# Two weight splits, one wide matmul: the FFNs of a four-block float32 stack with both operand parts in one 512-column matmul

## The chip, the core and the metric

The kernel runs on one core of a Trainium2 chip. The metric is the device time of one execution in microseconds. All work is in float32 accuracy, made out of matmuls on a reduced-precision operand type (float32r).

## The reference

Two blocks of two layers each, on 256 tokens of width 1024. Every layer is a mixer (retention with pooling, conformer convolution, short convolution, windowed attention) and then a SwiGLU FFN of inner width 2816:

```python
def swiglu(h, w_gate, w_up, w_down):
    return (jax.nn.silu(h @ w_gate) * (h @ w_up)) @ w_down

for layer in range(DEPTH):
    hn = rms_norm(h, mixer_norm_g[layer])
    h = h + mixer(hn, ...)
    h = h + swiglu(rms_norm(h, ffn_norm_g[layer]), ffn_w_gate[layer], ffn_w_up[layer], ffn_w_down[layer])
```

There are four FFNs in all; the change concerns them.

## The kernel before

**Layout.** Activations stand transposed: 128 features on the partitions, 256 tokens on the free axis; `h` has 8 such pieces, the FFN's inner activations 22. Weights come in tiles of 128x128, and all weights of the program lie in one array in the order in which they are used, 2944 tiles; 528 of them belong to each FFN: 352 for gate and up, 176 for down.

**Three products per tile.** A float32 product is made of three float32r ones. A weight piece (8 tiles, 1024 columns) arrives by DMA, ScalarE rounds it to `hi_t` (`split_hi`, L278), VectorE writes the rest, raw minus hi, to `lo_t` (`split_lo`, L284). An activation is split likewise, into `xh` (ScalarE, L305) and `xl` (VectorE, L309), inside an FFN into `fh` (L508) and `fl` (L469). `tile` issues three 256-column matmuls into one half of a PSUM bank: hi weight by high activation (L353), hi weight by low activation (L356), lo weight by high activation (L359). The lo by low product is left out.

**An FFN.** Up: group u (of 22) is 16 tiles, gate part in the first half of a bank and up part in the second, banks 0, 1, 6, 2 in turn (`UP_BANKS`). The first two groups are worked through together, by k. VectorE evicts a group with one 128x512 multiply by the broadcast of the RMS norm (L480), which frees the bank (semaphore `s_up`); ScalarE takes silu of the gate half (L516); VectorE multiplies by the up half (L465, called `gate`); ScalarE rounds to `fh` (L508, `high`); VectorE makes `fl` (L469, `low`), one group later. Down: block n (of 8) is 22 tiles, one for each inner piece, banks 3, 4, 5 in turn; VectorE adds the bank to `h` (L494), and the splits and squares for the next stage follow (L305, L309, L334). Out of these come the column sums (a small matmul into bank 7, `RMS_BANK`), the mean (L402), a power on GpSimd (L409), two diagonals (L415) and a broadcast matmul, due at tile 44 of the next FFN.

**What sets the order.** Everything is written out by hand: each engine runs its own program, and semaphores join them. `lo_to(e, c)` and `hi_to(e, c)` issue the splits that are due by tile c, so that a lo piece is issued about 3 pieces ahead of its use and a hi piece about 4; the ring of split pieces has 6 places, the ring of raw chunks (2 pieces, 1 MB) 3. GpSimd does little: powers, a few window sums and memsets. All weight DMAs are issued by SyncE.

Of the kernel before, what the change touches and what calls it, by code (L numbers as in the profile page):

```python
# [13 lines left out]
P = 128  # L14
# [158 lines left out]
def model_kernel(nc, w, poolw, xT, pos, cols, rows, consts, out):  # L173
    ctx = ExitStack()
    with ctx:
# [9 lines left out]
        h = sb("h", [P, KD, T])  # L185
        xh = sb("xh", [P, KD, T], F32R)
        xl = sb("xl", [P, KD, T], F32R)
        fh = sb("fh", [P, KF, T], F32R)
        fl = sb("fl", [P, KF, T], F32R)
        cst = sb("cst", [P, NCONST])  # L190
# [153 lines left out]

        def tile(e, g, dst, k, hi, lo, first, last, arrives=None):
# [7 lines left out]
            e.matmul(dst, hi_t[:, slot, c], hi[:, k, :], start=first, stop=False, skip_group_check=True)  # L353
            if arrives:
                e.wait_ge(*arrives[1])
            e.matmul(dst, hi_t[:, slot, c], lo[:, k, :], start=False, stop=False, skip_group_check=True)  # L356
            if r == 0:
                e.wait_ge(s_lo, g // 8 + 1)
            m = e.matmul(dst, lo_t[:, slot, c], hi[:, k, :], start=False, stop=last, skip_group_check=True)  # L359
            if g in MARKS:  # L360
                m.then_inc(s_tiles, 1)
# [30 lines left out]
        def pe_col_sums(e, i):  # L392
            ps = banks[:, RMS_BANK, :]
            e.wait_ge(s_ssum, squares_in(i))
            for n, sums in enumerate((ssum, ssum2)[:2 if i == 4 else 1]):
                for a in range(2):
                    m = plain(e, ps[:, 2 * n + a:2 * n + a + 1], sums[:, a * P:(a + 1) * P], one[:, 0:1])
            m.then_inc(s_col_sums, 1)

        def dve_mean(e, i):  # L400
            e.wait_ge(s_col_sums, i + 1)
            m = e.tensor_scalar(st[:, 0, :], banks[:, RMS_BANK, 0:2], 1.0 / D, EPS, ALU.mult, ALU.add)  # L402
            if i == 4:
                m = e.tensor_scalar(st[:, 2, :], banks[:, RMS_BANK, 2:4], 1.0 / D, None, ALU.mult)
            m.then_inc(s_mean, 1)
# [11 lines left out]
        def pe_spread(e, i):  # L417
            n = 4 if i == 4 else 2
            e.wait_ge(s_dg, DG_AT[i] + n)
            plain(e, banks[:, RMS_BANK, 0:n * P], one[:, :],  # L420
                  dg4[:, 0:n, :].rearrange("p a b -> p (a b)")).then_inc(s_spread, 1)

        def dve_rbc(e, i):
            e.wait_ge(s_spread, RBC_AT[i] + 1)
            e.tensor_copy(rbc[:, :], banks[:, RMS_BANK, 0:T]).then_inc(s_rbc, 1)
            e.wait_ge(s_rbc, RBC_AT[i] + 1)

        s_up, s_silu, s_gated = sem("up"), sem("silu"), sem("gated")  # L430
        t_ring = [scratch(n * 512, 512) for n in range(3)]
        s_ring = [scratch(1536 + n * T, T) for n in range(2)]
        m_ring = [scratch(2048 + n * T, T) for n in range(2)]

        def pe_ffn(e, f):
            i, g0, s = 2 * f + 1, G_FFN[f], 2 * f + 1
            for k in range(KD):
                for v in range(WIDE):
                    for t in range(2):
                        tile(e, g0 + 4 * k + 2 * v + t, banks[:, UP_BANKS[v], t * T:(t + 1) * T], k, xh, xl,  # L440
                             k == 0 and t == 0, k == KD - 1, x_of(i, k) if v == 0 and t == 0 else None)
            for u in range(WIDE, KF):
                if u >= len(UP_BANKS):
                    e.wait_ge(s_up, KF * f + u - len(UP_BANKS) + 1)
                for t in range(2):
                    for k in range(KD):
                        c = 16 * u + 8 * t + k
                        if c == 32:
                            pe_col_sums(e, i)
                        if c == 44:  # L450
                            pe_spread(e, i)
                        tile(e, g0 + c, banks[:, UP_BANKS[u % 4], t * T:(t + 1) * T], k, xh, xl, k == 0, k == KD - 1)
            for n in range(KD):
                if n >= 3:
                    e.wait_ge(s_h, h_done(i + 1, n - 3))
                for k in range(KF):
                    tile(e, g0 + UP_TILES + KF * n + k, banks[:, DOWN_BANKS[n % 3], 0:T], k, fh, fl, k == 0,
                         k == KF - 1, f_of(s, k) if n == 0 else None)

        def dve_ffn(e, f):  # L460
            i, g0, s = 2 * f + 1, G_FFN[f], 2 * f + 1

            def gate(u):
                e.wait_ge(s_silu, KF * f + u + 1)
                e.tensor_tensor(m_ring[u % 2], s_ring[u % 2], t_ring[u % 3][:, T:2 * T], ALU.mult).then_inc(s_gated, 1)  # L465
# [6 lines left out]
            dve_mean(e, i)  # L472
            dve_dg(e, i)
            lo_to(e, g0 + 44)
# [12 lines left out]
            gate(KF - 1)  # L487
            lo_to(e, g0 + UP_TILES + 19)
            low(KF - 1)
            for n in range(KD):  # L490
                c = g0 + UP_TILES + KF * (n + 1)
                lo_to(e, c)
                e.wait_ge(s_tiles, upto(c - 1))
                e.tensor_tensor(h[:, n, :], banks[:, DOWN_BANKS[n % 3], 0:T], h[:, n, :], ALU.add).then_inc(s_h, 1)  # L494
                if i + 1 < 8:
# [5 lines left out]
                    dve_square(e, i + 1, n)  # L501

        def act_ffn(e, f):
            i, g0, s = 2 * f + 1, G_FFN[f], 2 * f + 1

            def high(u):
                e.wait_ge(s_gated, KF * f + u + 1)
                e.activation(fh[:, u, :], m_ring[u % 2], ACT.Copy).then_inc(s_fh, 1)  # L508

            for u in range(KF):  # L510
                c = g0 + max(16 * (u + 1), 44)
                hi_to(e, c)
                e.wait_ge(s_up, KF * f + u + 1)
# [3 lines left out]
                hi_to(e, c + 3)  # L517
                if u:
# [20 lines left out]
        def pe_out_block(e, s, g0, n_outer, order, j, n):  # L539
            dst = banks[:, OUT_BANKS[j // 2], (j % 2) * T:(j % 2 + 1) * T]  # L540
            tile(e, out_tile(g0, n_outer, j, n), dst, order[n], fh, fl, n == 0 and j % 2 == 0, n == KD - 1,
                 f_of(s, n) if j == 0 else None)
# [137 lines left out]
        def pe_retention(e):  # L680
            for u in range(4):
                for t in range(2):
                    for k in range(KD):
# [3 lines left out]
                        if c == 46:  # L687
                            pe_spread(e, 0)
                        tile(e, G_QK + c, banks[:, u, t * T:(t + 1) * T], k, xh, xl, k == 0, k == KD - 1,
                             x_of(0, k) if c < KD else None)  # L690
            for k in range(KD):
                strip(e, G_V + 4 * k, (banks[:, 4, :], banks[:, 5, :]), k, k == 0, k == KD - 1)
            for u in range(2):
                e.wait_ge(s_qk, u + 1)
                for t in range(2):
                    for k in range(KD):
                        tile(e, G_U + 16 * u + 8 * t + k, banks[:, u, t * T:(t + 1) * T], k, xh, xl, k == 0, k == KD - 1)
            for u in range(2):
                e.wait_ge(s_qk, u + 3)
                for t in range(2):  # L700
                    for k in range(KD):
                        c = 16 * u + 8 * t + k
                        tile(e, G_G + c, banks[:, 2 + u, t * T:(t + 1) * T], k, xh, xl, k == 0, k == KD - 1)
                        if c % 8 == 3:
# [219 lines left out]
        def pe_conformer(e):  # L924
            for u in range(KD):
                if u >= len(UP_BANKS):
                    e.wait_ge(s_cup, u - len(UP_BANKS) + 1)
                for t in range(2):
                    for k in range(KD):
# [3 lines left out]
                        if c == 20:  # L933
                            pe_spread(e, 2)
                        tile(e, G_PW1 + c, banks[:, UP_BANKS[u % 4], t * T:(t + 1) * T], k, xh, xl, k == 0, k == KD - 1,
                             x_of(2, k) if c < KD else None)
# [152 lines left out]
        def pe_short(e):  # L1089
            for u in range(16):  # L1090
# [4 lines left out]
                for t in range(2 - u % 2):  # L1095
                    for k in range(KD):
# [594 lines left out]
```

## Time and profile before

| | |
|---|---|
| median of 3 runs | 1203.58 us (1201.99 to 1203.69) |
| the profiled execution | 1202.35 us, span 1200.5 us |
| TensorE matmul busy | 1177.2 us, 98%, 9228 instructions |
| VectorE busy | 811.6 us, 68% |
| ScalarE busy | 589.2 us, 49% |
| GpSimd busy | 30.7 us, 3% |
| DMA | 197.91 MB, mean 165 GB/s |

A busy share of TensorE says that something is in flight, not how fast it goes: matmuls overlap, and one of 0.28 us starts every 0.12. Its rate is read from start times or from the count in a window. The duration that the trace gives for one instruction of VectorE or ScalarE includes some latency, so back-to-back ones start closer together than they are long.

### The profile page before, as it was taken

How to read it: one execution, taken by the hardware profiler on the slowest of the kernel's cores; microseconds unless marked ns; L12 is line 12 of the kernel's file. 1: busy time of each engine (PE TensorE's matmuls, PEld its weight loads, DVE VectorE, ACT ScalarE, POOL GpSimd, SP SyncE). 2: the span in 40 equal slices, each digit the busy share in tenths (PEclk: the TensorE clock that was granted, in tenths of full speed). 3: DMA queues.
4: the chain of work that ended last, by engine and by line, in shares of the span. 5: the costliest groups of instructions: out<-in, count | busy, mean ns of one | idle time of the engine just before them, and what ended most of it. 6: DMA issues, size and time to landing. Idle time of an engine off the chain costs nothing.

```text
span 1200.5 us, 22339 instructions
## 1 busy us (share of the span) xinstructions
PE 1177.2 (98%) x9228; PEld 1142.8 (95%) x9228; DVE 811.6 (68%) x1302; ACT 589.2 (49%) x965; POOL 30.7 (3%) x54
## 2 busy tenths in 40 slices
PE   8999999999999799999999999999999899999999
PEld 8999999999998699999999999999998569999999
DVE  6867766655899577666656967666554897766642
ACT  6535444444745464445543545444444566544531
POOL 0120000000000000000000000000001200000000
PEclk8999999999999799999999999999999999999999
DMA  7543555555222045555543645555553323555551
GB/s 293 211 141 140 176 176 181 193 189 176 106 106 71 28 184 180 188 192 182 180 169 142 222 170 195 186 176 178 209 176 141 140 72 140 177 180 191 192 181 66
DMA packets 29046, 197.91 MB, mean 165 GB/s; under 512 B 3472, under 2 KB 4752, under 8 KB 5520
## 3 DMA queue, kind: packets, MB, share of 16 engines
q1 hardware_dynamic: 28656, 196.34, 45.7%
q8 instruction: 73, 1.20, 0.4%
q14 instruction: 29, 0.24, 0.1%
q10 hardware_dynamic: 288, 0.14, 0.0%
HBM read 195.41 MB, written 1.05 MB: 164 GB/s over the span
## 4 chain that ended last, share of the span: by engine, by line
PE 96%; DVE 2%; ACT 1%; DMA 0%; issue 0%; POOL 0%; DVEq 0%; ACTq 0%
PE banks L353 28%; PE banks L356 28%; PE banks L359 28%; PE banks L390 7%; PE banks L373 1%; PE banks L379 1%; PE banks L376 1%; DMA col<-cols 0%; PE banks L1276 0%; DVE scr L1493 0%; POOL scr L900 0%; DVE lo_t L284 0%; DVE scr L1476 0%; ACT scr L1337 0%; DVE scr L1481 0%
## 5 line engine op out<-in xcount | busy, mean ns | idle before, releaser
L353 PE MATMUL banks<-xh,hi_t 128*128 128x256 f32 x1856 | 530.0, 286 | 2.2 <-ACT hi_t L278 2.2
L359 PE MATMUL banks<-xh,lo_t 128*128 128x256 f32 x1856 | 526.3, 284 | 0.5 <-DVE lo_t L284 0.5
L356 PE MATMUL banks<-xl,hi_t 128*128 128x256 f32 x1856 | 526.3, 284 | 0.0
L284 DVE TENSOR_TENSOR lo_t<-raw_t,hi_t 128x1024 fp32r<-128x1024 f32 x368 | 444.8, 1221 | 12.2 <-ACT hi_t L278 7.7
L278 ACT ACTIVATE hi_t<-raw_t 128x1024 fp32r<-128x1024 f32 x368 | 380.6, 1048 | 71.2 <-PE banks L359 48.3
L353 PEld LDWEIGHTS banks<-xh,hi_t 128*128 128x128 f32 x1856 | 357.3, 192 | 3.0 <-ACT hi_t L278 2.4
L359 PEld LDWEIGHTS banks<-xh,lo_t 128*128 128x128 f32 x1856 | 357.3, 192 | 0.8 <-DVE lo_t L284 0.8
L356 PEld LDWEIGHTS banks<-xl,hi_t 128*128 128x128 f32 x1856 | 357.3, 193 | 0.6 <-issue 0.2
L353 PE MATMUL banks<-fh,hi_t 128*128 128x256 f32 x960 | 274.8, 286 | 4.8 <-ACT fh L1000 3.3
L356 PE MATMUL banks<-fl,hi_t 128*128 128x256 f32 x960 | 272.7, 284 | 0.5 <-DVE fl L840 0.4
L359 PE MATMUL banks<-fh,lo_t 128*128 128x256 f32 x960 | 272.3, 284 | 0.0
L353 PEld LDWEIGHTS banks<-fh,hi_t 128*128 128x128 f32 x960 | 184.9, 193 | 10.4 <-issue 10.4
L356 PEld LDWEIGHTS banks<-fl,hi_t 128*128 128x128 f32 x960 | 185.0, 193 | 1.4 <-DVE fl L840 0.6
L359 PEld LDWEIGHTS banks<-fh,lo_t 128*128 128x128 f32 x960 | 184.9, 193 | 0.0
L480 DVE TENSOR_TENSOR scr<-banks,rbc 128x512 f32<-128x512 f32 x88 | 60.4, 691 | 145.6 <-PE banks L359 145.4
L516 ACT ACTIVATE scr<-scr 128x256 f32<-128x256 f32 x88 | 36.8, 418 | 239.9 <-DVE scr L480 239.9
L494 DVE TENSOR_TENSOR h<-banks,h 128x256 f32<-128x256 f32 x32 | 13.6, 425 | 113.6 <-PE banks L359 113.6
L390 PE MATMUL banks<-scr 128*128 128x256 f32 (+4 forms) x368 | 76.7, 376 | 3.2 <-issue 1.5
L390 PEld LDWEIGHTS banks<-scr 128*128 128x128 f32 (+2 forms) x368 | 58.1, 183 | 16.3 <-issue 4.5
L305 ACT ACTIVATE xh<-h,col 128x256 fp32r<-128x256 f32 x56 | 26.1, 504 | 83.1 <-DVE h L494 66.7
L1062 DVE SCALAR_TENSOR_TENSOR scr<-scr,col 128x256 f32<-128x256 f32 x120 | 48.2, 480 | 0.0
L508 ACT ACTIVATE fh<-scr 128x256 fp32r<-128x256 f32 x88 | 36.8, 418 | 10.0 <-DVE scr L465 2.3
(160 smaller groups left out, 660.8 us busy)
## 6 DMA issues: line engine op xcount, KB each, us to landing
raw_t<-w SPq DMA_DIRECT2D x183, 1024.0 KB, 4.8
raw_t<-w SPq DMA_DIRECT2D x2, 512.0 KB, 7.0
out<-h SPq DMA_DIRECT2D x8, 128.0 KB, 3.7
cst<-consts SPq DMA_DIRECT2D x1, 800.0 KB, 11.1
h<-xT SPq DMA_DIRECT2D x1, 768.0 KB, 7.3
h<-xT SPq DMA_DIRECT2D x1, 256.0 KB, 4.2
pw<-poolw SPq DMA_DIRECT2D x1, 256.0 KB, 13.1
col<-cols SPq DMA_DIRECT2D x1, 193.0 KB, 8.1
```

The lines of the kernel that those rows point to most:

```text
L278: e.activation(hi_t[:, p % RING, :], raw_of(p), ACT.Copy).then_inc(s_hi, 1)
L284: e.tensor_tensor(lo_t[:, p % RING, :], raw_of(p), hi_t[:, p % RING, :].bitcast(F32), ALU.subtract).then_inc(s_lo, 1)
L305: e.activation(xh[:, k, :], h[:, k, :], ACT.Copy, scale=gain(i, k)).then_inc(s_xh, 1)
L353: e.matmul(dst, hi_t[:, slot, c], hi[:, k, :], start=first, stop=False, skip_group_check=True)
L356: e.matmul(dst, hi_t[:, slot, c], lo[:, k, :], start=False, stop=False, skip_group_check=True)
L359: m = e.matmul(dst, lo_t[:, slot, c], hi[:, k, :], start=False, stop=last, skip_group_check=True)
L390: return e.matmul(dst, lhs, rhs, start=start, stop=stop, skip_group_check=True)
L480: e.tensor_tensor(halves(t_ring[u % 3]), halves(banks[:, UP_BANKS[u % 4], :]), stretch(rbc[:, :], 1, 2), ALU.mult).then_inc(s_up, 1)
L494: e.tensor_tensor(h[:, n, :], banks[:, DOWN_BANKS[n % 3], 0:T], h[:, n, :], ALU.add).then_inc(s_h, 1)
L508: e.activation(fh[:, u, :], m_ring[u % 2], ACT.Copy).then_inc(s_fh, 1)
L516: e.activation(s_ring[u % 2], t_ring[u % 3][:, 0:T], ACT.Silu).then_inc(s_silu, 1)
L1062: last[n % 2] = dv.mark(e.scalar_tensor_tensor(acc[n % 2], src, wk, acc[n % 2], ALU.mult, ALU.add))
```

## The change

Activations' high and low parts now lie side by side: `x2` and `f2` of shape [128, pieces, 2, 256], and `xh`, `xl`, `fh`, `fl` are views into them. In the four FFNs `broad_tile` takes the place of `tile`: one 512-column matmul of the hi tile over both parts into a whole bank, so that the hi-by-high sum grows in the bank's first half and the hi-by-low sum in its second, then the 256-column lo matmul into the first half. The two halves are added at eviction. Other stages keep the three matmuls. The rest follows from whole banks:

- An up group takes a pair of banks, (0, 1), (6, 7), (4, 5) in turn, where it took one of four. Down takes banks 3, 7, 6; the norm's bank is 2 in front of FFNs.
- ScalarE copies the pair's second halves to SBUF (`side`, 128x512), VectorE adds the first halves (`add`, 128x512, frees the pair), then scales by the norm in place, in SBUF (128x512).
- The gate by up multiply goes from VectorE to GpSimd (`pool_ffn`), 22 per FFN.
- The residual add is two adds of 128x256, the second waiting for the first.
- On ScalarE `hi_to(c + 3)` goes ahead of silu. The first two `add`s come before and after the norm's diagonals.
- A broad tile that waits for an activation waits for both parts ahead of its one hi matmul.

```diff
+PAIRS = (0, 6, 4)
+DOWN_BANKS = (3, 7, 6)
...
+def rms_bank(i):
+    return 2 if i % 2 else RMS_BANK
...
+        x2 = sb("x2", [P, KD, 2, T], F32R)
+        f2 = sb("f2", [P, KF, 2, T], F32R)
+        xh, xl, fh, fl = x2[:, :, 0, :], x2[:, :, 1, :], f2[:, :, 0, :], f2[:, :, 1, :]
...
+        def broad_tile(e, g, bank, k, parts, first, last, arrives=None):
+            slot, r = piece(e, g)
+            c = slice(r * P, (r + 1) * P)
+            if r == 0:
+                e.wait_ge(s_hi, g // 8 + 1)
+            if arrives:
+                e.wait_ge(*arrives[0])
+                e.wait_ge(*arrives[1])
+            e.matmul(halves(banks[:, bank, :]), hi_t[:, slot, c], parts[:, k, :, :], start=first, stop=False,
+                     skip_group_check=True)
+            if r == 0:
+                e.wait_ge(s_lo, g // 8 + 1)
+            m = e.matmul(banks[:, bank, 0:T], lo_t[:, slot, c], parts[:, k, 0, :], start=False, stop=last,
+                         skip_group_check=True)
...
+            def add(u):
+                e.wait_ge(s_side, KF * f + u + 1)
+                if u >= 3:
+                    e.wait_ge(s_gated, KF * f + u - 2)
+                e.tensor_tensor(halves(t_ring[u % 3]), pair_of(u, 0), halves(b_ring[u % 2]), ALU.add).then_inc(s_up, 1)
...
                 lo_to(e, c)
-                e.wait_ge(s_tiles, upto(g0 + 16 * max(u, 1) + 15))
-                e.tensor_tensor(halves(t_ring[u % 3]), halves(banks[:, UP_BANKS[u % 4], :]), stretch(rbc[:, :], 1, 2),
-                                ALU.mult).then_inc(s_up, 1)
+                if u >= WIDE:
+                    add(u)
+                both = halves(t_ring[u % 3])
+                e.wait_ge(s_up, KF * f + u + 1)
+                e.tensor_tensor(both, both, stretch(rbc[:, :], 1, 2), ALU.mult).then_inc(s_scaled, 1)
                 lo_to(e, c + 3)
                 if u:
-                    gate(u - 1)
...
-                e.tensor_tensor(h[:, n, :], banks[:, DOWN_BANKS[n % 3], 0:T], h[:, n, :], ALU.add).then_inc(s_h, 1)
+                ps = banks[:, DOWN_BANKS[n % 3], :]
+                m = dv.mark(e.tensor_tensor(h[:, n, :], ps[:, 0:T], h[:, n, :], ALU.add))
+                e.wait_ge(dv.sem, m)
+                e.tensor_tensor(h[:, n, :], ps[:, T:2 * T], h[:, n, :], ALU.add).then_inc(s_h, 1)
...
+        def pool_ffn(e, f):
+            for u in range(KF):
+                e.wait_ge(s_silu, KF * f + u + 1)
+                if u >= 2:
+                    e.wait_ge(s_fl, f_done(2 * f + 1, u - 2))
+                e.tensor_tensor(m_ring[u % 2], s_ring[u % 2], t_ring[u % 3][:, T:2 * T], ALU.mult).then_inc(s_gated, 1)
...
+            def side(u):
+                e.wait_ge(s_tiles, upto(g0 + 16 * max(u, 1) + 15))
+                if u >= 2:
+                    e.wait_ge(s_up, KF * f + u - 1)
+                e.activation(halves(b_ring[u % 2]), pair_of(u, 1), ACT.Copy).then_inc(s_side, 1)
```

VectorE in the first FFN, before: one up group in the middle of the stage (eviction, split, gate, split, low half) and the eviction of the next.

```order
134 L480 TENSOR_TENSOR scr<-banks,rbc 128x512 [waits tiles]
135 L284 TENSOR_TENSOR lo_t<-raw_t,hi_t 128x1024 [waits hi,tiles]
136 L465 TENSOR_TENSOR scr<-scr 128x256 [waits silu]
137 L284 TENSOR_TENSOR lo_t<-raw_t,hi_t 128x1024 [waits hi,tiles]
138 L469 TENSOR_TENSOR fl<-scr,fh 128x256 [waits fh]
139 L480 TENSOR_TENSOR scr<-banks,rbc 128x512 [waits tiles]
```

VectorE at the same place now: add of the halves (L501), scaling (L517), two splits, low half (L495, here into `f`), and the next add.

```order
142 L501 TENSOR_TENSOR scr<-banks,scr 128x512 [waits gated,side]
143 L517 TENSOR_TENSOR scr<-scr,rbc 128x512 [waits up]
144 L290 TENSOR_TENSOR lo_t<-raw_t,hi_t 128x1024 [waits hi,tiles] x2
145 L495 TENSOR_TENSOR f<-scr,f 128x256 [waits fh]
146 L501 TENSOR_TENSOR scr<-banks,scr 128x512 [waits gated,side]
```

The wait for the tiles has moved to ScalarE's copy, of which the add waits, and the gate is gone from between the splits.

ScalarE in the first FFN, one up group before (silu L516, rounding to the high half L508, hi splits L278) and the next silu.

```order
116 L516 ACTIVATE scr<-scr 128x256 [waits gated,up]
117 L278 ACTIVATE hi_t<-raw_t 128x1024 [waits tiles,raw1]
118 L508 ACTIVATE fh<-scr 128x256 [waits gated]
119 L278 ACTIVATE hi_t<-raw_t 128x1024 [waits tiles,raw1]
120 L516 ACTIVATE scr<-scr 128x256 [waits gated,up]
```

ScalarE there now: the copy of the second halves (L558), a split, silu (L572), high half (L552), a split.

```order
129 L558 ACTIVATE scr<-banks 128x512 [waits up,tiles]
130 L284 ACTIVATE hi_t<-raw_t 128x1024 [waits tiles,raw1]
131 L572 ACTIVATE scr<-scr 128x256 [waits gated,scaled]
132 L552 ACTIVATE f<-scr 128x256 [waits gated]
133 L284 ACTIVATE hi_t<-raw_t 128x1024 [waits tiles,raw1]
```

One split now stands ahead of silu, and the copy ahead of both.

## Rows read from the trace of the kernel before

**Rows 1.** The page: TensorE's busy time, and the chain by engine.
```profile
PE 1177.2 (98%) x9228; PEld 1142.8 (95%) x9228; DVE 811.6 (68%) x1302; ACT 589.2 (49%) x965; POOL 30.7 (3%) x54
...
PE 96%; DVE 2%; ACT 1%; DMA 0%; issue 0%; POOL 0%; DVEq 0%; ACTq 0%
```

**Rows 2.** Waits of TensorE, longest first: total, times, longest us.
```profile
PE banks L353 <- ACT fh L1000: 3.3, 1, 3.3
```

**Rows 3.** Windows: stretch, its us, busy (x matmuls), granted clock, DMA share, GB/s.
```profile
130.00:230.00 100.00, 100.00 (x836) 1.00 0.54 190
```

**Rows 4.** Timeline of TensorE: start us, us, engine, line, operation, operands.
```profile
35.71 0.40 PE L373 MATMUL banks<-hi_t,xh 128*128 128x512 f32 x1
...
43.89 0.39 PE L373 MATMUL banks<-hi_t,xh 128*128 128x512 f32 x1
...
46.61 0.28 PE L353 MATMUL banks<-xh,hi_t 128*128 128x256 f32 x1
46.73 0.28 PE L356 MATMUL banks<-xl,hi_t 128*128 128x256 f32 x1
...
234.98 0.28 PE L353 MATMUL banks<-fh,hi_t 128*128 128x256 f32 x1
```

**Rows 5.** Timeline of VectorE, last up group of the first FFN.
```profile
235.18 0.69 DVE L480 TENSOR_TENSOR scr<-banks,rbc 128x512 f32<-128x512 f32 x1 [2.00 <-PE banks L359]
235.79 1.22 DVE L284 TENSOR_TENSOR lo_t<-raw_t,hi_t 128x1024 fp32r<-128x1024 f32 x1
236.92 0.42 DVE L465 TENSOR_TENSOR scr<-scr 128x256 f32<-128x256 f32 x1
237.38 1.23 DVE L284 TENSOR_TENSOR lo_t<-raw_t,hi_t 128x1024 fp32r<-128x1024 f32 x1
238.52 0.42 DVE L469 TENSOR_TENSOR fl<-scr,fh 128x256 fp32r<-128x256 f32 x1
...
240.32 0.42 DVE L469 TENSOR_TENSOR fl<-scr,fh 128x256 fp32r<-128x256 f32 x1
```

**Rows 6.** Groups by line and form: count, busy us, mean ns, idle before.
```profile
L804 DVE TENSOR_TENSOR scr<-scr 128x512 f32<-128x512 f32 x4 | 2.8, 692 | 0.1
L801 DVE TENSOR_TENSOR scr<-banks,scr 128x512 f32<-128x512 f32 x4 | 2.7, 686 | 0.1
...
L278 ACT ACTIVATE hi_t<-raw_t 128x1024 fp32r<-128x1024 f32 x368 | 380.6, 1048 | 71.2 <-PE banks L359 48.3 <-DMA raw_t<-w 15.7 <-PE banks L379 5.4
L516 ACT ACTIVATE scr<-scr 128x256 f32<-128x256 f32 x88 | 36.8, 418 | 239.9 <-DVE scr L480 239.9
...
L1361 ACT ACTIVATE scr<-banks,col 128x512 f32<-128x512 f32 x2 | 1.3, 686 | 0.2 <-PE banks L1255 0.2
```

**Rows 7.** Timelines of VectorE and GpSimd in the retention stage.
```profile
48.14 2.35 DVE L284 TENSOR_TENSOR lo_t<-raw_t,hi_t 128x1024 fp32r<-128x1024 f32 x2
...
53.17 2.79 DVE L284 TENSOR_TENSOR lo_t<-raw_t,hi_t 128x1024 fp32r<-128x1024 f32 x2
...
53.40 1.49 POOL L891 TENSOR_TENSOR scr<-scr 128x271 f32<-128x271 f32 x1 [25.78 <-issue]
...
56.01 0.63 POOL L891 TENSOR_TENSOR scr<-scr 128x271 f32<-128x271 f32 x1
```

**Rows 8.** Timelines of TensorE and VectorE, end of the first FFN.
```profile
298.34 0.28 PE L353 MATMUL banks<-xh,hi_t 128*128 128x256 f32 x1
...
298.54 0.42 DVE L494 TENSOR_TENSOR h<-banks,h 128x256 f32<-128x256 f32 x1 [2.80 <-PE banks L359]
...
299.54 0.48 DVE L309 SCALAR_TENSOR_TENSOR xl<-h,col,xh 128x256 fp32r<-128x256 f32 x1 [0.58 <-ACT xh L305]
```

**Rows 9.** Timeline of VectorE, its last instruction.
```profile
1197.75 0.42 DVE L494 TENSOR_TENSOR h<-banks,h 128x256 f32<-128x256 f32 x1 [7.49 <-PE banks L359]
```

**Rows 10.** Timeline of VectorE, the norm early in the first FFN.
```profile
119.47 0.16 DVE L402 TENSOR_SCALAR st<-banks 128x2 f32<-128x2 f32 x1 [2.66 <-PE banks L390]
120.44 0.48 DVE L415 TENSOR_SCALAR dg<-cst,st 128x128 f32<-128x128 f32 x2 [0.81 <-POOL st L409]
```

More of the change, by code:

```diff
@@ L343, in piece, with tile @@
             return p % RING, r
-        def tile(e, g, dst, k, hi, lo, first, last, arrives=None):
+        def tile(e, g, dst, k, parts, first, last, arrives=None):
             slot, r = piece(e, g)
@@ L419, in pe_spread @@
             e.wait_ge(s_dg, DG_AT[i] + n)
-            plain(e, banks[:, RMS_BANK, 0:n * P], one[:, :],
+            plain(e, banks[:, rms_bank(i), 0:n * P], one[:, :],
                   dg4[:, 0:n, :].rearrange("p a b -> p (a b)")).then_inc(s_spread, 1)
@@ L424, in dve_rbc @@
             e.wait_ge(s_spread, RBC_AT[i] + 1)
-            e.tensor_copy(rbc[:, :], banks[:, RMS_BANK, 0:T]).then_inc(s_rbc, 1)
+            e.tensor_copy(rbc[:, :], banks[:, rms_bank(i), 0:T]).then_inc(s_rbc, 1)
             e.wait_ge(s_rbc, RBC_AT[i] + 1)
-        s_up, s_silu, s_gated = sem("up"), sem("silu"), sem("gated")
+        s_side, s_up, s_scaled, s_silu, s_gated = sem("side"), sem("up"), sem("scaled"), sem("silu"), sem("gated")
         t_ring = [scratch(n * 512, 512) for n in range(3)]
@@ L433, in model_kernel, with pair_of @@
         m_ring = [scratch(2048 + n * T, T) for n in range(2)]
+        b_ring = [scratch(2560 + n * 512, 512) for n in range(2)]
+        def pair_of(u, half):
+            return banks[:, PAIRS[u % 3]:PAIRS[u % 3] + 2, half * T:(half + 1) * T]
         def pe_ffn(e, f):
@@ L451, in pe_ffn @@
                             pe_spread(e, i)
-                        tile(e, g0 + c, banks[:, UP_BANKS[u % 4], t * T:(t + 1) * T], k, xh, xl, k == 0, k == KD - 1)
+                        broad_tile(e, g0 + c, PAIRS[u % 3] + t, k, x2, k == 0, k == KD - 1)
             for n in range(KD):
@@ L512, in act_ffn @@
                 hi_to(e, c)
-                e.wait_ge(s_up, KF * f + u + 1)
+                if u >= WIDE:
+                    side(u)
+                hi_to(e, c + 3)
+                e.wait_ge(s_scaled, KF * f + u + 1)
                 if u >= 2:
@@ L540, in pe_out_block @@
             dst = banks[:, OUT_BANKS[j // 2], (j % 2) * T:(j % 2 + 1) * T]
-            tile(e, out_tile(g0, n_outer, j, n), dst, order[n], fh, fl, n == 0 and j % 2 == 0, n == KD - 1,
+            tile(e, out_tile(g0, n_outer, j, n), dst, order[n], f2, n == 0 and j % 2 == 0, n == KD - 1,
                  f_of(s, n) if j == 0 else None)
@@ L688, in pe_retention @@
                             pe_spread(e, 0)
-                        tile(e, G_QK + c, banks[:, u, t * T:(t + 1) * T], k, xh, xl, k == 0, k == KD - 1,
+                        tile(e, G_QK + c, banks[:, u, t * T:(t + 1) * T], k, x2, k == 0, k == KD - 1,
                              x_of(0, k) if c < KD else None)
@@ L696, in pe_retention @@
                     for k in range(KD):
-                        tile(e, G_U + 16 * u + 8 * t + k, banks[:, u, t * T:(t + 1) * T], k, xh, xl, k == 0, k == KD - 1)
+                        tile(e, G_U + 16 * u + 8 * t + k, banks[:, u, t * T:(t + 1) * T], k, x2, k == 0, k == KD - 1)
             for u in range(2):
@@ L702, in pe_retention @@
                         c = 16 * u + 8 * t + k
-                        tile(e, G_G + c, banks[:, 2 + u, t * T:(t + 1) * T], k, xh, xl, k == 0, k == KD - 1)
+                        tile(e, G_G + c, banks[:, 2 + u, t * T:(t + 1) * T], k, x2, k == 0, k == KD - 1)
                         if c % 8 == 3:
@@ L934, in pe_conformer @@
                             pe_spread(e, 2)
-                        tile(e, G_PW1 + c, banks[:, UP_BANKS[u % 4], t * T:(t + 1) * T], k, xh, xl, k == 0, k == KD - 1,
+                        tile(e, G_PW1 + c, banks[:, UP_BANKS[u % 4], t * T:(t + 1) * T], k, x2, k == 0, k == KD - 1,
                              x_of(2, k) if c < KD else None)
```

47 lines of the change are left out of this document (24 added, 23 removed).

## The prediction

> **What bounds the kernel now.** First the share of busy time and the chain of waits: TensorE is busy 98% of the span and makes 96% of the chain that ended last [rows 1]. Second, the waits of TensorE: the longest is 3.3 us, in the stage between two FFNs [rows 2], and none of its 17 rows is a wait for the up eviction (L480), the gate (L465), its halves (L508, L469) or the residual add (L494). Third, the spacing of its matmuls, which a busy share can't tell because matmuls overlap: a 100 us window inside the first FFN holds 836 of them at a granted clock of 1.00, that is 2.4 GHz, and in the timeline they start 0.12 us apart [rows 3, 4]. So the FFN stages are a gapless stream: a weight tile costs three starts, 0.36 us, and 528 tiles make 190 us, four times. What shortens that stream shortens the kernel until another engine falls behind it.
>
> **The two matmuls made one.** The FFNs have 4 x 528 = 2112 tiles. In each, the two 256-column matmuls on the high weight tile become one of 512 columns; the third stays. The trace of before has 512-column matmuls of the same number type, in the V projection: 48 of them run from 35.71 to 46.61 us, 0.2271 us each, and the last twelve, from 43.89 to 46.61, take 0.2267 each [rows 4]. The matmul at 46.61 is one of 256 columns, and the next follows 0.12 later: at the seam each matmul is paid by its own length. Twice the columns cost 0.107 us more, not 0.12: about 13 ns are paid per matmul whatever its length, and the change takes one such share from each tile. By the mean of 48: 0.2400 - 0.2271 = 12.9 ns, times 2112 = 27.2 us. By the last twelve: 13.3 ns, 28.2 us. I take 27.7. The operand differs from the strips' (there the weights stream and the activations stand), but its 512 columns lie side by side as theirs do.
>
> The Trainium skill, "TensorE: Matmul & The Clock Gate", section "Back-to-back issue gap", gives an isolated spacing of columns over 2.4 GHz plus about 2.5 ns. By that rule the share saved would be an estimated 2.5 ns, the sum 5.3 us and the time 1198.7, on the side of rival 2 below; the rows above disagree with it (0.12 for 256 columns, where it has 0.109), and the measurement decides.
>
> **The eviction of a group (16 tiles).** A group takes TensorE 16 x 0.36 = 5.76 us now, and 16 x 0.347 = 5.55 then. VectorE starts L480, two lo splits (L284), the gate and the low half at intervals of 0.61, 1.13, 0.46 and 1.14, and 0.42 for the last: 3.8 us, then it waits 2 us for TensorE [rows 5]. After: the add of the halves (reads PSUM) and the scaling (SBUF alone), both 128x512 and 0.69 long as L801 and L804 are [rows 6]; the scaling at its full 0.69 because it waits for the first; two splits 2.26; low half 0.34; no gate. Sum 4.0 us of 5.55. ScalarE gets a 512-column copy out of PSUM; the nearest row is its other PSUM one, 0.69 (L1361) [rows 6]. Its group was 2 x 1.05 for the hi splits and 2 x 0.42 [rows 6]; with 0.69 it comes to 3.6 of 5.55. Both have room, so I cost the added work at nothing; the cover is TensorE's stream, and without it each us per group would cost 88 us over the 88 groups. The moved order matters little: the lo split of a piece that follows the eviction of group u is read 24 tiles, 8.3 us, later, and the pair of banks is wanted two groups, 11.1 us, later (three pairs in place of four banks), while copy plus add are through 1.4 us after the group's last matmul. Of DMAs the change moves none; weights are wanted 4% faster, from a share of 0.54 [rows 3].
>
> **The gate on GpSimd.** A 128x271 add takes it 0.63 us undisturbed, and the gate's 256-column multiply is of that kind. One that started inside two lo splits of VectorE took 1.49, and the pair of splits 2.79 in place of 2.35 [rows 7]: whoever shares costs GpSimd 0.86 and VectorE 0.44. The group budget of VectorE then is 4.0 + 0.44 = 4.5 (bound from the other side: it stands still for all of a 1.49 gate, 5.5), still within 5.55. I take 4.5, the measured case.
>
> The Trainium skill, "SBUF — State Buffer", section "Who interferes with whom", says that a VectorE instruction with two SBUF inputs and a GpSimd one that reads SBUF exclude each other for a whole instruction; the trace agrees in kind, and by that rule in full the gate would wait at most one split.
>
> **From up to down.** The first down block needs the last gated tile (number 21) 21 tiles after it starts. Before, down starts at 234.98, VectorE writes the last low half at 240.32 + 0.42 = 240.74, and TensorE wants it at 234.98 + 21 x 0.36 = 242.5: 1.8 us spare [rows 4, 5]. After, counted from down's start: copy and its signal 0.8, add 0.7, scaling 0.7, two splits 2.26, low half 20 0.34, one more split 1.13, low half 21 0.42: 6.35, with the contention above 6.8. Wanted at 21 x 0.347 = 7.3. Spare 0.5 us: nothing lost, but this is the narrow place. ScalarE has its high half 21 ready by about 5: silu ends at 2.65, the gate at 3.3 to 4.2, high half 0.42.
>
> **From down to the next stage and the end.** The residual add is now two dependent adds, 0.42 more. At the end of the first FFN the chain L494, L305, L309 ends at 299.54 + 0.48 = 300.02, and the next stage wants it seven tiles after 298.34, at 300.86 [rows 8]: 0.84 spare, 0.42 then, so nothing at the three inner ends. At the kernel's end nothing covers it: last matmul, L494, output [rows 9]; +0.42 us once. Early in an FFN the order on VectorE puts the first add between mean and dg; the mean ran at 119.47 and dg at 120.44 with a wait for GpSimd between [rows 10], so half the add fits in it, and the spread is due 4.2 us after the column sums. Nothing.
>
> **Sum.** Profiled execution 1202.35 us (span 1200.5): -27.7 + 0.4 = 1175.1. The median of the runs, 1203.58, lies 1.2 above that execution; against it I forecast 1176.3.
>
> **Rivals.**
> 1. The conversion tail is late. If GpSimd's gate 21 gets no turn until VectorE's three splits are done (about 5.7 us after down starts), it ends at 6.35, high half at 6.8, low half at 7.3 to 7.8 with signals, against a need at 7.3; with each of three splits lengthened as in [rows 7] (0.2) it is 8.4. TensorE then stands 0.5 to 1.1 us in each of four FFNs: 1178 to 1181. For it: the split pair in [rows 7] held GpSimd back. Against: in those rows GpSimd did get its turn within the pair.
> 2. The 512-column matmul does not run at the strips' spacing in this mix, for instance 0.235 in place of 0.227: 5 ns x 2112 = 10.6 us are saved, 1193. At the end of it, 0.24, there is no gain and only the 0.42 stays: the change then does not do what it says. Against it: the seam at 46.61 in [rows 4].
> 3. Slower: VectorE becomes the bound in the up groups, in the place where its lo splits meet the gate. The gain of the down blocks, 8 x 22 x 4 = 704 tiles x 13 ns = 9.2 us, is kept, so a group must take 5.76 + (9.2 - 0.4)/88 = 5.86 us to eat it. That is an interference of 1.86 us per gate over the 4.0 us; at 2.3 us (group 6.3) the time is 1203.6 + 48 - 9 = 1243. The rows show 0.44, and a stop for the whole gate 1.49; both are below the point.
>
> **Chances.** Forecast 0.80; its own range is 1174.5 to 1178. Rival 1: 0.13. Rival 2: 0.04. Rival 3: 0.03. The range has to reach the tail's stalls, 1181, and a little of other waits in four stages: 1173.8 to 1182.5. No change is within 0.2%, 2.4 us, about what measurements of this kernel can tell; only the far end of rival 2 is there: faster 0.96, same 0.01, slower 0.03.
>
> **What the profile after would show.** TensorE: starts 0.227 and 0.12 apart, 144 pairs in 50 us, and an FFN of 183 us. Its waits: none on the low halves at the start of down; a row there of about 1 us, four times, is rival 1. VectorE: a wait of about 1 us before each add, waiting for ScalarE's copy; if that is gone and TensorE waits for lo splits, rival 3. GpSimd: 88 multiplies between 0.65 and 1.5 us, with splits of up to 1.6 us beside them. A total above 1185 would make the forecast wrong, and the spacing of pairs tells at once whether the matmul or a wait is the cause.

## The result, and the profile after

The changed kernel takes 1188.86 us (1188.42 to 1189.44, 4 runs) against 1203.55 in the same comparison: ratio 0.9881, 95% interval 0.9864 to 0.9898. It is 14.7 us faster. 1176.3 was forecast, 27.3 us faster, with a range that ended at 1182.5: the direction is right, but the forecast saving is 1.9 times the measured one. (The kernel before was measured again beside each later group of runs: 1202.4 to 1202.8 us.)

The page of the changed kernel: busy time by engine, the chain by engine, and the costliest groups (line, engine, operation, operands, count, busy us, mean ns, idle before).

```profile
PE 1161.8 (98%) x7116; PEld 1028.4 (87%) x7116; DVE 893.4 (75%) x1334; ACT 631.2 (53%) x1053; POOL 132.8 (11%) x142
...
PE 95%; DVE 3%; ACT 1%; DMA 1%; issue 0%; POOL 0%; SPq 0%; DVEq 0%; ACTq 0%
...
L290 DVE TENSOR_TENSOR lo_t<-raw_t,hi_t 128x1024 fp32r<-128x1024 f32 x368 | 481.5, 1340 | 8.4 <-ACT hi_t L284 7.0
...
L545 POOL TENSOR_TENSOR scr<-scr 128x256 f32<-128x256 f32 x88 | 102.1, 1162 | 363.4 <-ACT scr L572 363.4
L558 ACT ACTIVATE scr<-banks 128x512 f32<-128x512 f32 x88 | 52.1, 597 | 153.0 <-PE banks L383 153.0
```

The answer to [rows 1]: TensorE is still the bound, with 2112 fewer matmuls. Its waits, longest first (total, times, longest us), the answer to [rows 2]:

```profile
PE banks L359 <- ACT f L1055: 3.3, 1, 3.3
PE banks L1331 <- DVE scr L1448: 3.0, 1, 3.0
PE banks L359 <- ACT hi_t L284: 2.7, 1, 2.7
```

The largest is the same 3.3 us as before, and none of the 17 rows of that view waits for the new copy, add, scaling, gate or residual adds. So the missing 12.6 us are not in a wait for the added work. The window and the timeline of TensorE, answers to [rows 3, 4]:

```profile
130.00:230.00 100.00, 100.00 (x567) 1.00 0.53 190
```

```profile
150.29 0.40 PE L379 MATMUL banks<-x,hi_t 128*128 128x512 f32 x1
150.52 0.28 PE L383 MATMUL banks<-x,lo_t 128*128 128x256 f32 x1
150.64 0.40 PE L379 MATMUL banks<-x,hi_t 128*128 128x512 f32 x1
150.88 0.28 PE L383 MATMUL banks<-x,lo_t 128*128 128x256 f32 x1
151.00 0.40 PE L379 MATMUL banks<-x,hi_t 128*128 128x512 f32 x1
...
151.35 0.40 PE L379 MATMUL banks<-x,hi_t 128*128 128x512 f32 x1
```

Three pairs from 150.29 to 151.35 are 0.353 each; start times over 50 us stretches in all four FFNs give 0.3532 to 0.3534, and 567 matmuls in 100 us say the same. Forecast was 0.347. The saving per tile is 0.3600 - 0.3533 = 6.7 ns, times 2112 = 14.1 us; less the 0.42 at the end that is 13.7, against 13.8 us by which the span fell (1200.5 to 1186.7). Of the pair, the wide matmul has 0.236 until the next start and the narrow one 0.117 (means from 130 to 230 us; the trace holds whole nanoseconds, which the view rounds).

### The profile page after: what moved, and what is told of

Same layout as the page of the kernel before. It is cut to its first block, busy times and chain, and to the rows that moved or that the text cites. A ratio compares the mean times of both kernels' runs of the same rounds, so it can differ in the third digit from the quotient of the medians.

```text
span 1186.7 us, 18655 instructions
## 1 busy us (share of the span) xinstructions
PE 1161.8 (98%) x7116; PEld 1028.4 (87%) x7116; DVE 893.4 (75%) x1334; ACT 631.2 (53%) x1053; POOL 132.8 (11%) x142
## 4 chain that ended last, share of the span: by engine, by line
PE 95%; DVE 3%; ACT 1%; DMA 1%; issue 0%; POOL 0%; SPq 0%; DVEq 0%; ACTq 0%
PE banks L379 42%; PE banks L383 21%; PE banks L415 8%; PE banks L359 7%; PE banks L362 7%; PE banks L365 7%; PE banks L398 1%; PE banks L404 1%; PE banks L401 1%; DMA h<-xT 1%; DVE lo_t L290 1%; PE banks L1331 0%; DVE scr L1548 0%; POOL scr L955 0%; ACT x L311 0%
## 5 line engine op out<-in xcount | busy, mean ns | idle before, releaser
L379 PE MATMUL banks<-x,hi_t 128*128 128x512 f32 x1408 | 498.6, 399 | 0.0
L290 DVE TENSOR_TENSOR lo_t<-raw_t,hi_t 128x1024 fp32r<-128x1024 f32 x368 | 481.5, 1340 | 8.4 <-ACT hi_t L284 7.0
L383 PE MATMUL banks<-x,lo_t 128*128 128x256 f32 x1408 | 395.3, 281 | 0.0
L379 PEld LDWEIGHTS banks<-x,hi_t 128*128 128x128 f32 x1408 | 264.6, 188 | 65.3
L383 PEld LDWEIGHTS banks<-x,lo_t 128*128 128x128 f32 x1408 | 266.0, 189 | 0.1
L379 PE MATMUL banks<-f,hi_t 128*128 128x512 f32 x704 | 248.9, 399 | 0.0
L383 PE MATMUL banks<-f,lo_t 128*128 128x256 f32 x704 | 197.7, 281 | 0.0
L379 PEld LDWEIGHTS banks<-f,hi_t 128*128 128x128 f32 x704 | 132.3, 188 | 33.1
L545 POOL TENSOR_TENSOR scr<-scr 128x256 f32<-128x256 f32 x88 | 102.1, 1162 | 363.4 <-ACT scr L572 363.4
L558 ACT ACTIVATE scr<-banks 128x512 f32<-128x512 f32 x88 | 52.1, 597 | 153.0 <-PE banks L383 153.0
L383 PEld LDWEIGHTS banks<-f,lo_t 128*128 128x128 f32 x704 | 133.0, 189 | 0.0
L359 PE MATMUL banks<-x,hi_t 128*128 128x256 f32 x448 | 129.9, 290 | 2.7 <-ACT hi_t L284 2.7
L365 PE MATMUL banks<-x,lo_t 128*128 128x256 f32 x448 | 127.5, 285 | 1.2 <-DVE lo_t L290 1.2
L362 PE MATMUL banks<-x,hi_t 128*128 128x256 f32 x448 | 127.5, 285 | 0.0
L501 DVE TENSOR_TENSOR scr<-banks,scr 128x512 f32<-128x512 f32 x88 | 60.8, 691 | 77.9 <-ACT scr L558 77.3
L359 PEld LDWEIGHTS banks<-x,hi_t 128*128 128x128 f32 x448 | 86.4, 193 | 3.5 <-ACT hi_t L284 2.9
L365 PEld LDWEIGHTS banks<-x,lo_t 128*128 128x128 f32 x448 | 86.5, 193 | 1.6 <-DVE lo_t L290 1.6
L362 PEld LDWEIGHTS banks<-x,hi_t 128*128 128x128 f32 x448 | 86.5, 193 | 0.5 <-issue 0.2
L529 DVE TENSOR_TENSOR h<-banks,h 128x256 f32<-128x256 f32 x32 | 13.6, 425 | 91.5 <-PE banks L383 91.5
## 6 DMA issues: line engine op xcount, KB each, us to landing
pw<-poolw SPq DMA_DIRECT2D x1, 256.0 KB, 13.5
```

Of the source, the lines that this page charges most:

```text
L290: e.tensor_tensor(lo_t[:, p % RING, :], raw_of(p), hi_t[:, p % RING, :].bitcast(F32), ALU.subtract).then_inc(s_lo, 1)
L359: e.matmul(dst, hi_t[:, slot, c], parts[:, k, 0, :], start=first, stop=False, skip_group_check=True)
L362: e.matmul(dst, hi_t[:, slot, c], parts[:, k, 1, :], start=False, stop=False, skip_group_check=True)
L365: m = e.matmul(dst, lo_t[:, slot, c], parts[:, k, 0, :], start=False, stop=last, skip_group_check=True)
L379: e.matmul(halves(banks[:, bank, :]), hi_t[:, slot, c], parts[:, k, :, :], start=first, stop=False, skip_group_check=True)
L383: m = e.matmul(banks[:, bank, 0:T], lo_t[:, slot, c], parts[:, k, 0, :], start=False, stop=last, skip_group_check=True)
```

## The experiments

Eleven kernels ran, runs 7, 8 and 9 once each, the others four times. "Wide" is a 512-column matmul, "narrow" the 256-column one. The question is why a pair costs 6.6 ns more than a wide and a narrow matmul do in streams of one width (0.2267 + 0.1200 = 0.3467). The first theories came from one stretch of the trace, the first two up groups of the first FFN, which ran at the forecast rate. There TensorE's timeline of the changed kernel reads:

```profile
108.00 0.40 PE L379 MATMUL banks<-x,hi_t 128*128 128x512 f32 x1
...
109.04 0.39 PE L379 MATMUL banks<-x,hi_t 128*128 128x512 f32 x1
```

Three tiles in 1.04 us, 0.347 each. These groups run k outermost: their tiles change the bank at every tile and share the moving operand over four. Elsewhere the bank stays and the operand changes.

**1. Change the bank at every tile.**

```diff
+UP_ORDER = [(t, k) for k in range(KD) for t in range(2)]
...
-                for t in range(2):
-                    for k in range(KD):
-                        c = 16 * u + 8 * t + k
...
+                for at, (t, k) in enumerate(UP_ORDER):
+                    c = 16 * u + at
...
```

> Up groups from the third on run k outermost, so that successive tiles alternate between the pair's two banks and two of them share a moving operand (weights are laid out in that order; the result is the same). In the changed kernel a pair of matmuls (512 + 256) takes 0.3472 us in the first two up groups and 0.3533 everywhere else. Theory B (a 512-column matmul pays about 6 ns when the matmul before it wrote the same bank) and theory A (when it wrote the same columns): 0.347 in up, 0.353 in down, total 1188.9 - 1280 x 6.1 ns = 1181. Theory M (a 512-column matmul pays when its moving operand differs from that of the matmul before it): half of the tiles are free of it, 0.350 in up, 1185. Theory S (the sizes alternate, nothing else): 0.353, 1188.9.

Measured: 1188.57 us, 0.3533 per tile in up. No change.

**2. Change bank and operand at every tile.** The rest of the edit is as in run 1.

```diff
+UP_ORDER = [((k + s) % 2, k) for s in range(2) for k in range(KD)]
```

> As the run before, but bank and moving operand both change at every tile of an up group: (gate, 0), (up, 1), (gate, 2), ... and then the other eight. Theories B and A: 0.347 in up, 1181. Theory M: 0.353 in up, 1188.9. Theory S: 1188.9.

Measured: 1188.68 us, 0.3532 to 0.3534. No change.

**3. The lo matmul adds to other columns.**

```diff
-            m = e.matmul(banks[:, bank, 0:T], lo_t[:, slot, c], parts[:, k, 0, :], ...
+            m = e.matmul(banks[:, bank, T:2 * T], lo_t[:, slot, c], parts[:, k, 0, :], ...
```

> The order of before, but the 256-column matmul of the lo weights adds into the second half of its bank (columns 256 to 511) in all FFN tiles; the sum of the halves is the same. Theory A (same columns as the 512-column matmul begins with): 0.347 everywhere, total 1188.9 - 2112 x 6.1 ns = 1177 at the most. Theory B (same bank is enough), M and S: 0.353, 1188.9.

Measured: 1189.16 us, 0.3532 to 0.3536. And the first two up groups of the first FFN, where the order is as it was, now show 0.3533 too; the timeline of run 3 there:

```profile
108.54 0.40 PE L379 MATMUL banks<-x,hi_t 128*128 128x512 f32 x1
...
109.60 0.40 PE L379 MATMUL banks<-x,hi_t 128*128 128x512 f32 x1
```

Three tiles in 1.06 us. So neither the bank, nor the columns, nor the operand sets the rate, and the 0.347 of those groups was not theirs: runs 1 to 4 have the same order there and show 0.353. The trace of the changed kernel could have told that at once: in its other three FFNs the same two groups, with the same program, run at 0.3534. The observation that the theories were made from does not repeat. What is left is the mix of widths, or the new operand layout.

**4. The gate back on VectorE.** `gate(u)` returns to `dve_ffn` between the two splits, and `pool_ffn` is not called.

> The gate times up multiply goes back to VectorE, 22 per FFN, between the two splits as before; all else as in the changed kernel. Prediction's view: TensorE is the bound and the added work is hidden, so within 0.2% of 1188.9; lo splits fall from a mean of 1.34 us to 1.22. Rival: the contention of GpSimd and VectorE is what ate the missing 12 us, then about 1177.

Measured: 1190.49 us (1190.40 to 1190.71). It is not faster but 1.6 us slower. The profiled span is 1.0 us longer (1187.7), and one wait of TensorE in the attention stage, 1.5 us in place of 0.3, is as large as that; run 3 shows this wait as well, with its gate on GpSimd. The splits fall as expected, from 1340 ns to:

```profile
L290 DVE TENSOR_TENSOR lo_t<-raw_t,hi_t 128x1024 fp32r<-128x1024 f32 x368 | 443.9, 1219 | 8.8 <-ACT hi_t L284 7.3
```

The contention is real, and hidden: the rival that wanted about 1177 is out.

**5 and 6. Sort the matmuls by width.** `broad_queue` collects tiles and `broad_run` issues them; a run ends at the end of a weight piece or of a block.

`AT_ONCE` is 2 in run 5 and 8 in run 6.

```diff
+            for n, (g, bank, k, parts, first, last, arrives) in enumerate(items):
...
+                e.matmul(halves(banks[:, bank, :]), hi_t[:, slot, c], parts[:, k, :, :], ...)
+            for n, (g, bank, k, parts, first, last, arrives) in enumerate(items):
...
+                m = e.matmul(banks[:, bank, 0:T], lo_t[:, slot, c], parts[:, k, 0, :], ...)
...
+                if len(items) == AT_ONCE or (item[0] + 1) % 8 == 0 or item[5]:
+                    broad_run(e, items)
```

> In all FFNs two tiles at a time: both 512-column matmuls, then both 256-column ones (same result). Theories A, B and M have fallen: the first two up groups now show 0.3533 too, with the same order in which they once showed 0.3472. Theory T (every change from a 256-column matmul to a 512-column one, or back, costs 6.7 ns): 0.350 us per tile, total 1188.9 - 2112 x 3.3 ns = 1182. Theory P (after 256-column matmuls the first four or five 512-column ones each take 0.2333 in place of 0.2267, as at the start of the V and Q projections): 0.3533, 1188.9. Theory O (a 512-column matmul out of this operand layout takes 0.2333 whatever its neighbours): 0.3533, 1188.9.

Measured: 1179.19 us (1178.80 to 1179.72), ratio 0.9807 (0.9792 to 0.9821) to the kernel before in the same comparison, and 9.7 us below the changed kernel in time and in span (1186.7 to 1177.0). The timeline of TensorE:

```profile
149.67 0.62 PE L401 MATMUL banks<-x,hi_t 128*128 128x512 f32 x2
150.13 0.40 PE L408 MATMUL banks<-x,lo_t 128*128 128x256 f32 x2
150.37 0.63 PE L401 MATMUL banks<-x,hi_t 128*128 128x512 f32 x2
...
151.76 0.63 PE L401 MATMUL banks<-x,hi_t 128*128 128x512 f32 x2
```

Six tiles from 149.67 to 151.76: 0.348 each. 5.0 ns x 2112 = 10.6 us, against 9.7 measured. The same number of wide matmuls out of the same layout goes faster when only their order changes, so the layout alone (theory O) is not it. P wanted 0.3533 here and misses too.

> As the run before with up to eight tiles at a time (a weight piece, shorter where a block of down ends): eight 512-column matmuls, then eight 256-column ones. Theory T: 6.7 ns per about eight tiles, 0.3475 per tile, total about 1177. Theory P: five of eight pay, 0.351, 1184. Theory O: 0.3533, 1188.9.

Measured: 1181.81 us; 0.3492 per tile (2.793 us for eight, by 38 such distances in the up groups of the first FFN; here 150.60 to 153.40):

```profile
150.60 2.00 PE L401 MATMUL banks<-x,hi_t 128*128 128x512 f32 x8
152.44 1.12 PE L408 MATMUL banks<-x,lo_t 128*128 128x256 f32 x8
153.40 2.00 PE L401 MATMUL banks<-x,hi_t 128*128 128x512 f32 x8
```

Theory T in its simple form wanted 0.3475, P 0.351: neither fits, and a quarter of the changes does not cost a quarter. But this trace shows where the excess lies. The eight wide matmuls take 1.84 us (150.60 to 152.44), not 8 x 0.2267 = 1.81: the first five have 0.228 to 0.236 each, 0.232 on the mean, and the last three exactly 0.2267. The first two narrow ones then take 0.113 and 0.119, the others 0.120. Five times 5.5 ns more and 7.6 ns less are the 20 ns that a round costs over 8 x 0.3467. The kernel before has the same steps at both ends of its V projection: 233, 236, 229, 232, 231 ns and then 227 behind narrow matmuls, 113, 119 and then 120 behind wide ones. So P is right in what it says of wide matmuls behind a run of narrow ones; it leaves out what the narrow ones give back.

**7. Wide matmuls alone.** In the first FFN the lo matmul also runs over both parts.

```diff
+            both = g < G_F0 + 528
...
+            if both:
+                m = e.matmul(halves(banks[:, bank, :]), lo_t[:, slot, c], parts[:, k, :, :], ...)
...
```

> In the first FFN the lo matmul is 512 columns wide too (it adds the lo by lo product, which the other kernels leave out), so that this FFN is a stream of 512-column matmuls alone. Theories T and P: 0.4533 us per tile there, FFN of 239 us, total 1188.9 + 528 x 0.100 = 1241.7. Theory O: 0.4667, total 1248.7.

Measured: 1244.06 us. The timeline:

```profile
149.82 0.39 PE L380 MATMUL banks<-x,hi_t 128*128 128x512 f32 x1
...
151.19 0.39 PE L380 MATMUL banks<-x,hi_t 128*128 128x512 f32 x1
151.41 0.39 PE L385 MATMUL banks<-x,lo_t 128*128 128x512 f32 x1
```

Six matmuls from 149.82 to 151.19 take 1.37 us; over the 100 us from 130 to 230 they are 0.2267 apart, 0.453 per tile. The first to the last hi matmul of that FFN are 239.9 us apart, the norm's small matmuls among them. In company of its own width the new matmul runs at the pace of the strips in [rows 4]. Theory O is out for good. (The total is 2.4 us above the sum; the trace puts that outside this FFN.)

**8. A narrower lo matmul.**

```diff
+            w = P if g < G_F0 + 528 else T
+            m = e.matmul(banks[:, bank, 0:w], lo_t[:, slot, c], parts[:, k, 0, 0:w], ...
```

> In the first FFN the lo matmul takes 128 columns in place of 256 (the correction of the last 128 tokens is left out there), the weight load before it stays. If a matmul costs its columns at 2.4 GHz and a fixed share, a tile takes 0.3533 - 0.0533 = 0.300 and the total falls by 28 us to 1161. Theory L (the 0.12 us of a 256-column matmul are the time of the weight load behind it, and its columns are hidden under that): 0.353, no change, 1189; a value between gives the length of the load.

Measured: 1183.57 us, 0.340 per tile in the first FFN (180.0 us from first to last wide matmul, against 187.0; the total fell by 5.3, so not all of that arrived at the end). Neither 0.300 nor 0.353. The timeline of the weight loads:

```profile
150.14 0.19 PEld L379 LDWEIGHTS banks<-x,hi_t 128*128 128x128 f32 x1
150.25 0.19 PEld L384 LDWEIGHTS banks<-x,lo_t 128*128 128x128 f32 x1
150.48 0.19 PEld L379 LDWEIGHTS banks<-x,hi_t 128*128 128x128 f32 x1
150.59 0.19 PEld L384 LDWEIGHTS banks<-x,lo_t 128*128 128x128 f32 x1
```

The two loads of a tile start 0.11 apart, and the next tile's 0.23 later; over 294 tiles from 130 to 230 us the means are 0.1083 and 0.2317. The first is more than 128 columns would take by the equal-width rule (0.0533 + 0.0133) and less than the 0.12 of 256 columns. Run 9 has the same 0.1083 between the loads with 192 and with 224 columns. So these weight loads do not follow one another closer than 0.108 us on the mean, whatever the width, and I read that as a floor for a matmul with a load of its own; a stream of such narrow matmuls alone was not run. The floor of 0.1133 in the expectation of run 9 is another reading: it is what is left of 0.340 when 0.2267 is taken off for the wide matmul, but the trace has 0.2317 between the loads there. The Trainium skill, "TensorE: Matmul & The Clock Gate", section "Back-to-back issue gap", says that load and matmul set the spacing together; this run agrees in kind: half the columns did not bring 0.300.

**9. Four more widths.**

```diff
+LO_WIDTHS = (192, 224, 288, 384)
...
+            w = LO_WIDTHS[sum(g >= at for at in G_FFN) - 1]
```

> The changed kernel with the lo matmul 192, 224, 288 and 384 columns wide in the first, second, third and fourth FFN (below 256 the correction of the last tokens is left out, above it some lo by lo products are added). Known so far, per tile: 128 columns 0.340, 256 columns 0.3533, 512 columns 0.4533. If a matmul costs columns over 2.4 GHz plus 13.3 ns, but at least the 0.1133 of the weight load that the 128-column run shows, the four take 0.340, 0.340, 0.360 and 0.400. Theory T (6.7 ns more for every alternation of widths): 0.347, 0.347, 0.367, 0.407. If only 256 columns pay, it is a matter of that length and not of alternation.

Measured: 1216.82 us. The last FFN's timeline:

```profile
1079.80 0.40 PE L381 MATMUL banks<-x,hi_t 128*128 128x512 f32 x1
1080.04 0.34 PE L385 MATMUL banks<-x,lo_t 128*128 128x384 f32 x1
1080.21 0.40 PE L381 MATMUL banks<-x,hi_t 128*128 128x512 f32 x1
...
1081.04 0.40 PE L381 MATMUL banks<-x,hi_t 128*128 128x512 f32 x1
```

Three pairs in 1.24 us: 0.413. All widths of the lo matmul beside a wide one, per tile in us, with the equal-width rule (columns over 2.4 GHz plus 0.0133 each, but at least the 0.1083 between the loads):

| lo columns | 128 | 192 | 224 | 256 | 288 | 384 | 512 |
|---|---|---|---|---|---|---|---|
| measured | 0.340 | 0.344 | 0.343 | 0.3533 | 0.364 | 0.413 | 0.453 |
| rule | 0.335 | 0.335 | 0.335 | 0.3467 | 0.360 | 0.400 | 0.4533 |
| excess, ns | 5 | 9 | 8 | 7 | 4 | 13 | 0 |

It is not a matter of 256 columns. All six mixed pairs pay 4 to 13 ns; the pair of equal widths pays nothing. The first three columns lean on the floor (with 0.1133 they would be 0, 4 and 3), the others do not. A fixed price per alternation (theory T) is not what it is: 256, 288 and 384 columns alone give 7, 4 and 13.

**10. Four at a time.** `AT_ONCE = 4`.

> Four 512-column matmuls, then four 256-column ones. One, two and eight at a time gave 0.3533, 0.348 and 0.3487 per tile. Theory T: 0.3483 at most, nearer 0.3475; total at or 1 us below the 1179.2 of two at a time. Theory P (each wide matmul after narrow ones pays up to the fifth): 0.350 to 0.353 and 1183 to 1189.

Measured: 1184.16 us, 0.351 per tile (twelve tiles from 150.66 to 154.87). Worse than two and than eight. T wanted at most 0.3483 and 1179.2 and fails; P wanted 0.350 to 0.353 and 1183 to 1189, and both came. Per round of n wide and n narrow ones the excess over n x 0.3467 is 6.7 ns for one, 3.3 for two, 17 for four and 20 for eight.

The steps at the V projection of the kernel before can be added up for each round (n wide ones of 233, 236, 229, 232, 231, then 227 ns; n narrow ones of 113, 119, then 120):

| tiles at a time | 1 | 2 | 4 | 8 |
|---|---|---|---|---|
| by those steps, us per tile | 0.346 | 0.3505 | 0.3505 | 0.349 |
| measured | 0.3533 | 0.3483 | 0.3508 | 0.3492 |

For four and eight the seam seen before accounts for the measurement; for one and two it does not, and there no run tells why.

**11. Two at a time, gate on VectorE.**

> Two at a time, with the gate multiply on VectorE. View of the prediction: TensorE is the bound, the place of the gate does not matter: 1179.2 within 2.4 us, lo splits at 1.22 us mean. Rival: the shorter stream makes the room of VectorE count, and it is slower by more than 2.4 us (or faster, if the contention with GpSimd was what counted).

Measured: 1180.30 us (1179.87 to 1182.38), against 1179.19 with the gate on GpSimd; the splits are 1.22 us. The same within 0.1%, as expected.

## Why the forecast was wrong, point by point

- **What bounds the kernel** (TensorE, by start spacing): right. TensorE stayed the bound in every run.
- **The two matmuls made one**: the failed step. "The change takes one such share from each tile" put 13.1 ns (12.9 to 13.3; 27.7 us in all) where 6.7 came (14.1 us). The wide matmul has the strips' pace among its like (run 7), the narrow one has its own, and their alternation has neither: 0.3533 for 0.3467. The error is 13.6 us, all of the miss, which is 13.5 by the spans and 12.6 by the medians. "About 13 ns are paid per matmul whatever its length" describes streams of one width and was carried over to a mix without a row for one.
- **"At the seam each matmul is paid by its own length"**: wrong, and a single seam was read as a rule for a stream of seams. At 46.61 the rounded start times show 0.12; in nanoseconds the first two narrow matmuls take 113 and 119. And the trace of before had a sign against it at the other seam. Its strips do not start at 0.2267; TensorE's timeline of the kernel before, at the other end of that stretch:

```profile
36.64 0.39 PE L376 MATMUL banks<-hi_t,xl 128*128 128x512 f32 x1
36.87 0.39 PE L379 MATMUL banks<-lo_t,xh 128*128 128x512 f32 x1
```

From 35.71 [rows 4] to 36.87 lie five spacings, 0.232 each, right behind the 256-column stream; the later ones are 0.2267. Averaged into 0.2271 over 48, that looked like noise; taken as the price of a wide matmul behind narrow ones it gives 0.232 + 0.120 = 0.352 per tile, 16.9 us saved, 1187.1. That comes near, but part of it is luck: by the same seam's first steps alone (233 + 113 ns) one pair would cost 0.346.
- **Rival 2** (the wide matmul does not run at the strips' spacing in this mix) is what happened, with 6.6 ns per pair where its example took 8; it was given 0.04, and the range did not reach it. The Trainium skill's isolated spacing ("TensorE: Matmul & The Clock Gate", "Back-to-back issue gap", columns over 2.4 GHz plus 2.5 ns) puts a pair at an estimated 0.325, much further from 0.3533 than the strips' 0.3467. The saving by it, 2.5 ns per tile and 1198.7 us, is off by less than the forecast's 13.1 ns and 1176.3 (6.7 ns and 1188.86 came), but as that rule has the pair wrong by 28 ns, this is luck.
- **Eviction at no cost**: right. VectorE waits 1.1 us for the copy in 72 of the 88 groups, as was said; ScalarE's copy takes 0.60, less than the 0.69 taken for it.
- **The gate on GpSimd**: right in kind. It takes 1.16 on the mean (0.65 to 1.5 said), and splits that meet it lengthen. VectorE and GpSimd in one group:

```profile
149.99 2.90 DVE L290 TENSOR_TENSOR lo_t<-raw_t,hi_t 128x1024 fp32r<-128x1024 f32 x2
...
150.60 1.21 POOL L545 TENSOR_TENSOR scr<-scr 128x256 f32<-128x256 f32 x1 [4.46 <-ACT scr L572]
```

The pair of splits takes 2.90 against 2.35 alone, 0.55 where 0.44 was taken. The rule of the Trainium skill ("SBUF — State Buffer", "Who interferes with whom") holds here: the gate ends at 151.81, 0.60 after the first split has ended at 151.20, and the second split is the one that is longer (1.77); by runs 4 and 11 it costs nothing that can be measured.
- **From up to down**: right, on the safe side. Down starts at 232.62 and the last low half ends at 239.49, 6.9 us later (6.8 said). It is wanted at 7.4 with the slower tiles; the forecast's 7.3 would also have done. Rival 1 did not happen: TensorE's waits have no row there. VectorE's last low half:

```profile
239.08 0.41 DVE L495 TENSOR_TENSOR f<-scr,f 128x256 fp32r<-128x256 f32 x1
```

- **The end**: right. The two adds follow one another there, 0.46 apart where 0.42 was taken, and the output after them:

```profile
1183.56 0.42 DVE L529 TENSOR_TENSOR h<-banks,h 128x256 f32<-128x256 f32 x1 [6.88 <-PE banks L383]
1184.02 0.42 DVE L531 TENSOR_TENSOR h<-banks,h 128x256 f32<-128x256 f32 x1
```

- **Open**: why a pair alternating at every matmul costs 6.7 ns, why other widths cost 4 to 13, and why two at a time is the best order tried. Shown is that the excess comes with the mix of widths and changes with the order alone, and for runs of four and eight that it lies in the first five wide matmuls behind narrow ones. The bank, the columns written, the order of the moving operands, the layout, the gate's engine and waits are excluded. Its mechanism inside TensorE no run here tells; in particular none leaves out a weight load, so a part of the loads in it is neither shown nor excluded. Nor is it explained why the first two up groups of one FFN once ran at 0.347.

The best version measured is the changed kernel with two tiles at a time (run 5): 1179.19 us, 23 below the kernel before in the same comparison and 10 below the changed one.

## What to carry to other kernels

Price a matmul in the company that it will keep: the spacing inside a run of equal matmuls does not add up to the spacing of a mix. If a kernel alternates widths, try the same matmuls sorted in twos; here that returned 10 us for an edit of order alone. When a forecast rests on one small difference times two thousand, look at the first instructions of the reference stretch as well as at its mean, and at every repetition of a stretch in the trace before a theory is built on one of them.

## What the runs showed of the hardware that was not expected

- Float32r matmuls at a granted clock of 1.00 with a weight load each: 0.2267 us for 512 columns and 0.1200 for 256 in streams of one width. Their loads did not start closer together than 0.108 on the mean, with 128, 192 and 224 columns alike (runs 8 and 9). Alternating 512 and 256: 0.3533 per pair, in place of 0.3467.
- At a seam between the widths the pace changes for several matmuls: the first five wide ones take 0.232 on the mean before 0.2267 is reached, the first two narrow ones 0.113 and 0.119 (kernel before and run 6).
- The excess is not monotonic: 6.7, 3.3, 17 and 20 ns per round for rounds of one, two, four and eight; 4 to 13 ns per pair over six narrower widths, none for equal ones.
- The same piece of program can hold another pace: 0.347 per pair in the first 30 tiles of the first FFN in the trace of the changed kernel, 0.3533 in its other FFNs and in run 4, whose TensorE program is the same. With one trace of each kernel it is not shown whether this belongs to the build or to the execution.
